# The third up tile of each FFN's first stage: from a direct product to seven block products

## The reference, cut to what matters

```python
def _swiglu(h, wg, wu, wd):
    return (jax.nn.silu(h @ wg) * (h @ wu)) @ wd

def pre(y, j):
    return _rmsnorm(y, P['norm_g'][l, j]) * (1 + mod[:, :, 3 * j + 1]) + mod[:, :, 3 * j]

x = x + 0.5 * mod[:, :, 2] * _swiglu(pre(x, 0), P['ffn_wg'][l, 0], P['ffn_wu'][l, 0], P['ffn_wd'][l, 0])
# ... the mixer ...
x = x + 0.5 * mod[:, :, 8] * _swiglu(pre(x, 2), P['ffn_wg'][l, 1], P['ffn_wu'][l, 1], P['ffn_wd'][l, 1])
```

## Time and profile before

| | |
|---|---|
| median of 3 runs | 2552.2 us |
| the profiled execution's own time | 2564.95 us |
| its span, first to last instruction | 2562.9 us |
| mean granted clock of PE | 0.989 |
| PE busy | 2490.7 us, 97% |
| DVE busy | 1643.7 us, 64% |
| POOL and ACT busy | 1044.1 us, 1026.4 us |
| PE waits longest for | DVE `x` at the start of the later up stages, 21.5 us in 8 waits |

### The profile page before, as it was taken

How to read it: one execution, slowest core, us unless ns; L and a number is a source line. 1 busy time by engine, 2 the same in 40 slices (tenths; PEclk the granted TensorE clock), 3 DMA queues, 4 the chain that set the end, 5 groups by cost and what they waited for, 6 DMA issues and landing times. The chain is left out here.

```text
span 2562.9 us, 59302 instructions
## 1 busy us (share of the span) xinstructions
PE 2490.7 (97%) x23874; PEld 2362.6 (92%) x23874; DVE 1643.7 (64%) x3406; ACT 1026.4 (40%) x1944; POOL 1044.1 (41%) x810
## 2 busy tenths in 40 slices
PE   6999999999999999999999999999999999999998
PEld 4999998999889989999999999989998899999998
DVE  5676584377883465858575848545788734859392
ACT  3434342323465233434343534333244632535251
POOL 4434346334323544344554343552343236334343
PEclk9999999999999999999999999999999999999999
DMA  7353435323213514423523433542232235222322
GB/s 268 124 179 127 163 104 199 145 68 107 96 45 114 198 67 132 163 85 107 204 101 99 154 122 132 200 183 68 68 103 68 74 100 182 73 93 92 107 91 91
DMA packets 111781, 313.57 MB, mean 122 GB/s; under 512 B 19036, under 2 KB 45706, under 8 KB 94106
## 3 DMA queue, kind: packets, MB, share of 16 engines
q1 hardware_dynamic: 102560, 290.60, 33.1%
q10 hardware_dynamic: 8970, 19.44, 2.1%
HBM read 299.56 MB, written 10.66 MB: 121 GB/s over the span
## 5 line engine op out<-in xcount | busy, mean ns | idle before, releaser
L1081 POOL TENSOR_TENSOR w_lo<-raw,w_hi 128x512 fp32r<-128x512 f32 x448 | 560.8, 1278 | 895.6 <-ACT w_hi L1183 895.6
L1088 POOL TENSOR_TENSOR w_lo<-raw,w_hi 128x512 fp32r<-128x512 f32 x228 | 324.5, 1437 | 477.2 <-ACT w_hi L1220 477.2
L2630 PE MATMUL bank<-h_hi,w_hi 128*128 128x260 f32 (+1 forms) x1312 | 379.5, 289 | 1.0 <-POOL w_lo L1081 0.5
L2776 PE MATMUL bank<-t_hi,w_hi 128*128 128x260 f32 x1216 | 348.9, 287 | 21.5 <-DVE x L2134 21.5
L1183 ACT CAST w_hi<-raw 128x1024 fp32r<-128x1024 f32 (+2 forms) x164 | 216.6, 1321 | 382.0 <-PE bank L2632 289.4
L2631 PE MATMUL bank<-h_hi,w_lo 128*128 128x260 f32 (+1 forms) x1312 | 368.9, 281 | 0.0
L2632 PE MATMUL bank<-h_lo,w_hi 128*128 128x260 f32 (+1 forms) x1312 | 368.7, 281 | 0.0
L2631 PE MATMUL bank<-mid_hi,w_lo 128*128 128x260 f32 x1232 | 348.7, 283 | 0.0
L2630 PE MATMUL bank<-mid_hi,w_hi 128*128 128x260 f32 x1232 | 348.7, 283 | 0.0
L2632 PE MATMUL bank<-mid_lo,w_hi 128*128 128x260 f32 x1232 | 347.4, 282 | 0.0
L2778 PE MATMUL bank<-t_hi,w_lo 128*128 128x260 f32 x1216 | 347.0, 285 | 0.0
(11 more groups left out here) (396 smaller groups left out, 6300.2 us busy)
## 6 DMA issues: line engine op xcount, KB each, us to landing
raw<-in_w SPq DMA_DIRECT2D x120, 1024.0 KB, 4.9
raw<-in_w SPq DMA_DIRECT2D x128, 512.0 KB, 4.1
ada_ring<-in_ada SPq DMA_DIRECT2D x68, 256.0 KB, 5.5
ada_ring<-in_ada SPq DMA_DIRECT2D x48, 320.0 KB, 5.3
raw<-in_w SPq DMA_DIRECT2D x32, 384.0 KB, 3.3
ada_ring<-in_ada SPq DMA_DIRECT2D x48, 192.0 KB, 5.2
ada_low<-in_ada SPq DMA_DIRECT2D x20, 256.0 KB, 5.2
out_y<-x ACTq DMA_DIRECT2D x4, 1040.0 KB, 14.7
```

The lines of the kernel that those rows point to most:

```text
L1081: last = pool.tensor_tensor(w_lo[j][:, cols], raw[j][:, cols], w_hi[j][:, cols].bitcast(F32), ALU.subtract)
L1088: pool.tensor_tensor(place(w_lo, l, stage, slot, piece), src, place(w_hi, l, stage, slot, piece).bitcast(F32), ALU.subtract).then_inc(sema ...
L2630: mm(out, wh(wb), xh(xb), start=(n == 0), stop=False)
L2776: mm(out, wh[:, cols], x_hi[:, k], start=(start and k == 0), stop=False, skip_group_check=not start)
```

## The change

The kinds of a head become D D S S S S. The third tile is now done in seven block products, and what these need must be ready one tile earlier: the four token sums, the tile's weight sums, their casts and low parts. The two direct tiles keep `w_hi` columns 1024 to 2047 and 0 to 1023; the third tile's blocks lie rotated by two places (`turn`), so that the first of them go where tile 0's weights were. Its first three products come in another order: `ROW_11` (which needs no token sum), `SUM_3`, `SUM_2`, in place of `SUM_2`, `ROW_11`, `SUM_3`. All S tiles of a head lie rotated, so that the last one's casts share places with the casts for the down stage that follows.

On ACT the first two token casts stand ahead of the first tile's silu, and the second tile carries the third tile's seven casts. On DVE the first tile carries three token sums, three of their low parts and three weight sums, and the second tile the rest. A wait on `t_ready` is added in `t_values`.

```diff
-UP_KIND = ("DDDSSS", "SSSSSSSS", "SSSSSSSS")
+UP_KIND = ("DDSSSS", "SSSSSSSS", "SSSSSSSS")
...
-            pairs = [1] * slots
+            pairs = [0] * slots
...
-            four = 3
+            four, turn = 1, 2 if stage[3] == "0" else 0
...
-                    four = 5 - four
-                    PLACE[key] = at = [(0, 0), (0, 1), (0, 3), (0, 2), (1, 0), (1, 1), (1, four)]
+                    four = 1 - four
+                    PLACE[key] = at = [(j, (i + turn) % 4) for j, i in ((0, 0), (0, 1), (0, 3), (0, 2),
+                                                                       (1, 0), (1, 1), (1, 2 + four))]
+                    EARLY[key] = order = (ROW_11, SUM_3, SUM_2) if turn and slot == 2 else (SUM_2, ROW_11, SUM_3)
...
                     if start and slot == 0:
-                        silu(0)
-                        silu(1)
...
                         t_head(l, f, 0)
+                        t_head(l, f, 1)
+                        silu(0)
+                        silu(1)
                         high(0)
                         high(1)
-                        t_head(l, f, 1)
+                        t_head(l, f, 2)
                     elif start and slot == 1:
+                        cast(l, stage, 2, SUM_2)
                         silu(0)
+                        cast(l, stage, 2, ROW_11)
                         silu(1)
-                        t_head(l, f, 2)
                         cast(l, stage, 2, SUM_1)
+                        cast(l, stage, 2, SUM_3)
+                        cast(l, stage, 2, ROW_22)
+                        cast(l, stage, 2, ROW_12)
                         high(0)
+                        t_head(l, f, 3)
+                        high(1)
                         cast(l, stage, 2, SUM_4)
-                        high(1)
...
                     dve.wait_ge(t_made, n + 3)
+                    dve.wait_ge(t_ready, n + 1)
...
                     if start and slot == 0:
                         t_values(l, f, 0)
                         t_values(l, f, 1)
+                        t_values(l, f, 2)
                         prod(0)
                         prod(1)
                         low(0)
                         low(1)
+                        sums(l, stage, 2, "sum1")
+                        sums(l, stage, 2, "sum2")
                         t_low(l, f, 0)
                         t_low(l, f, 1)
-                        t_values(l, f, 2)
+                        sums(l, stage, 2, "sum3")
+                        t_low(l, f, 2)
                     elif start and slot == 1:
-                        t_low(l, f, 2)
+                        lead("low2")
                         t_values(l, f, 3)
                         prod(0)
                         low(0)
+                        lead("low1")
+                        lead("low3")
                         prod(1)
+                        t_low(l, f, 3)
                         low(1)
+                        lead("sum4")
+                        lead("low4")
...
+                if EARLY[key][0] == ROW_11:
+                    row11_product()
+                    sum3_product()
+                    sum2_product()
+                else:
+                    sum2_product()
+                    row11_product()
+                    sum3_product()
```

More of the change, by code:

```diff
@@ L227, in plan_places @@
             kinds = UP_KIND[int(stage[3])]
[L228 removed]
+            pairs = [0] * slots
             for slot in reversed(range(slots - 1)):
[L230 to L231 removed]
+                pairs[slot] = 1 - pairs[slot + 1] if kinds[slot:slot + 2] == "DD" else 0
+            four, turn = 1, 2 if stage[3] == "0" else 0
             for slot, kind in enumerate(kinds):
@@ L780, in kind_of, with early @@
             return KIND.get((l, stage, slot))
+        def early(key, piece):
+            return 3 * SUMS_BEFORE[key] + 1 + EARLY[key].index(piece)
         def pair_cols(l, stage, slot):
@@ L1336, in ffn_up @@
                     else:
-                        act.wait_ge(early_full, 3 * sums + 2)
+                        act.wait_ge(early_full, early(key, ROW_11))
                         s.copy(p1[:], up_bank(0)).then_inc(p1_copied, 1)
@@ L2078, in ffn_up @@
                         lead("sum2")
-                        dve.wait_ge(early_full, 3 * before + 1)
+                        dve.wait_ge(early_full, early(key, SUM_2))
                         dve.wait_ge(p1_copied, before + 1)
                         v.tensor_tensor(u2[:], gate_bank(1), p1[:], ALU.add).then_inc(combined, 1)
-                        dve.wait_ge(early_full, 3 * before + 3)
+                        dve.wait_ge(early_full, early(key, SUM_3))
                         dve.wait_ge(combined, 5 * before + 1)
@@ L2784, in tokens, with sum2_product, row11_product, sum3_product @@
                     return h_hi[:, k0:k0 + 4, half(hf)], h_lo[:, k0:k0 + 4, half(hf)]
[L2786 to L2795, removed]
+                def sum2_product():
+                    pe.wait_ge(t_ready, t0 + 3)
+                    pe.wait_ge(sum_split, 4 * before + 1)
+                    take_main(3, use)
+                    piece_product(gate_bank(1), SUM_2, t_hi[:, 2], t_lo[:, 2], True, True).then_inc(early_full, 1)
+                def row11_product():
+                    pe.wait_ge(piece_split, lows + 1)
+                    take_main(0, use)
+                    piece_product(up_bank(0), ROW_11, *tokens(0, 0), True, True).then_inc(early_full, 1)
+                def sum3_product():
+                    pe.wait_ge(t_ready, t0 + 2)
+                    pe.wait_ge(sum_split, 4 * before + 3)
+                    take_main(1, use)
+                    piece_product(gate_bank(0), SUM_3, t_hi[:, 1], t_lo[:, 1], True, True).then_inc(early_full, 1)
+                if EARLY[key][0] == ROW_11:
[6 more added lines that the diff above has]
+                    sum3_product()
                 take_main(2, use)
```

12 lines of the change are left out of this document (5 added, 7 removed).

## The result

The changed kernel takes 2569.1 us (median of 7 runs, 2564.33 to 2574.58), the kernel before in the same session 2556.0 (7 runs): ratio 1.0050, 95% interval 1.0037 to 1.0064, so 9.5 to 16.4 us slower. Between the medians it is 13.1 us. The prediction was slower, 2563 against 2552.2.

What follows compares the result with a forecast made beforehand. PE, busy 97%, was taken as the bound, with DVE nearly as full in the heads. Waits less saving gave +8.6 us, clock +1.7: 2552.2 + 10.3 = 2562.5, put at 2563, range 2551 to 2574.

Steps and rivals of the forecast that it cites:

- the second wait: PE at `ROW_22` waits for DVE's `u3`: 1.1 us in the first, second and last head, 1.4 in the third.
- the heads' forecast sum: Net change over the four heads, waits less saving: 2.3, 1.3, 3.7 and 1.3 us, together +8.6 us.
- The saving: Third tile of each head: 84 matmuls instead of 96, 1.435 us a head, 5.74 us in four.
- DVE's stretch to `mid_lo`: From DVE's first products to the second tile's first `mid_lo`: 10.7 us plus 2.85 for POOL; PE 1.6 us late, last head.
- The place of the third token sum: On DVE its 1.65 us fills an existing 1.68 us wait, so the last head's products begin as before.
- Silu in the first and third head: Silu behind the token casts on ACT makes PE late at the second tile by 1.65 and 1.8 us.
- POOL costs DVE nothing: Rival: `mid_lo` comes 2.85 us sooner and the first wait goes in all heads; -1 us, 2551; chance 0.15.
- The clock falls in each head: Rival: PE at half clock after each head's last wait, 4 x 1.7 us more, splits at full length; 2568 to 2574; chance 0.15.
- The price of a split: Each POOL split in the second tile costs DVE 0.95 us, 2.85 for three; bounds 0 and 1.50.
- the reading of the rule beside it: By the skill's port rule each split would cost DVE its whole 1.50 us, about 2570 us; the forecast kept 0.95.
- `down`: Casts for the down stage come later but stay hidden with 1.5 us of cover; no wait of PE there.

Runs made afterwards that it cites:

- bank 0 early: Changed kernel with the second tile's first product and `mid_lo` on DVE, which free bank 0, moved ahead of the fourth token sum: 2571.1 us, ratio 1.0060.
- e9_dve_light: Changed kernel with silu before the token casts, POOL's third-tile splits at 32 of 512 columns, token sums' low parts at 104 of 1040: 2547.1 us, ratio 0.9969.
- e1_silu_first: Changed kernel with the first tile's two silu put back ahead of the two token casts: 2569.9 us, ratio 1.0050.
- e5_split_short: Changed kernel with POOL's three splits of each head's third tile cut to 32 of 512 columns: 2557.4 us, ratio 1.0008.
- modulation later: Changed kernel with silu ahead of the token casts and four modulation turns moved from tiles 0 and 1 to 3 and 4: 2568.1 us, ratio 1.0057.

## Why the prediction was right, and where it was not

- **Direction, cause and range: right; that the size came so near is in part luck.** Forecast +10.3 us, measured 9.5 to 16.4. The waits were forecast too small in three heads. The first head costs 2.4 us without the 2.3 of its start (forecast 2.3), with no stretch at half clock in it. The second and the last were forecast at 1.3 each: they cost 5.1 and 5.3 here, about 4 of it without the clock (see the second wait below), and 3.9 and 4.0 in the run with bank 0 early, where no stretch fell into them. The third costs 5.9 against 3.7; its stretch lies ahead of the wait at `ROW_11` and shortens that. So the heads' forecast sum of 8.6 stands against about 16 (an estimate from the rows of one execution, at the upper end of what the times allow), while half clock, counted at 1.7 in the sum, took no more from the whole than before (25.6 us against 27.3).
- **The saving: right**, 1.435 a head, shown where DVE has time (`e9_dve_light`).
- **DVE's stretch to `mid_lo`: right, a little short.** 13.55 was forecast, 14.5 measured: 2.85 of POOL against 3.06, and 10.7 bare against 11.45. I left out the scaling (0.20) and took overlaps that not every pair of rows has.
- **The place of the third token sum: wrong.** "The third token sum (1.65) goes into the wait of 1.68 ahead of them" rested on a wait that a half-clock stretch just ahead of the head had made in that execution. Without it the products begin 1.6 us later: hence silu late by 1.0 in the second and last head, where I had none, and 3.0 to 3.2 us at `ROW_11` instead of 1.6.
- **The second wait: right where it can be seen**, 1.45 and 1.85 us in the first and third head against 1.1 and 1.4. In the other two PE ran at half clock there. At full clock it would have been at `ROW_22` at 2222.45 + 5.74 = 2228.2. `u3` ended at 2230.65, but 1.00 us of that was DVE's own wait for the slower PE ahead of `u2`: at full clock `u3` ends near 2229.65, and PE waits about 1.5 us (an estimate). So some 1.1 of those 3.4 us of clock were a cost, and the rest was swallowed or lay in the wait ahead, as the forecast said of such a loss.
- **Silu in the first and third head: right** (1.7 and 2.0 against 1.65 and 1.8). It was right to let DVE's and PE's later times follow from it: `e1_silu_first` shows that it is a part of one lateness: without it the time is the same.
- **The rivals.** "POOL costs DVE nothing" fell with `e5_split_short`. "The clock falls in each head" was half right: in three of four, 8.5 us, but the profile as a whole lost no more to the clock (25.6 us) than that of before (27.3).
- **The price of a split: right (0.95 against 1.02); the reading of the rule beside it: wrong.** A DVE row of 128x512 beside a split ends 0.54 to 0.55 us behind it whenever the row began, so DVE loses what is left of the split when it comes: about 1.0 of 1.27 us here. The whole length would be lost only by an instruction that comes as the split begins; and the 1.50 put in for it is half of a row (3.00) in which POOL itself waits for DVE, as the 1.87 here does. The Trainium skill (SBUF — State Buffer, "Who interferes with whom") says that the later of the two is blocked completely. The trace agrees: held until the split's end, in all 339 rows, with 3.06 us lost to three.
- **`down`: right**, no wait there.

## What to carry to other kernels

When an engine off the bound has no gaps through a stage, price a change there by the work it has up to the point where it catches up. None of the five orders tried here took the delay away: they moved the wait of the bound engine to another instruction. A gap that is to take up new work should be looked for in a second profile first, and what the engine ahead of it did at which clock. A subtraction that POOL takes over may, where DVE has no gap, cost DVE more (1.02 us) than doing it itself (0.60).

## What the hardware showed that I had not expected

- What a POOL split takes from DVE is what is left of it when DVE's instruction comes, and not a share of that instruction's length: 1.0 to 1.1 us on a weight sum, on a `t_lo` (2.33 instead of 1.24, third head), and on a scaling of 72 columns that lasts 0.20 alone.
- Half clock comes with long waits in the heads. With the waits of 2.3 to 4.4 us at `ROW_11` in the changed kernel (second and last head), with silu first and with modulation later (all heads), ten in all, a stretch at 1.2 GHz began each time between 1.0 us before the wait's end and 0.7 behind it. With those of 2.6 to 3.0 us at `ROW_22` with bank 0 early it did so in the first and third head and not in the second and last. The silu wait of 1.8 us in the third head brought one in five runs of six, that of 1.6 in the first head in none of the same six. In the run with DVE light, which has no such waits, none fell into a head.
